# Moving the output projection, the second norm, the query products and the key scores between the two phases of units 1, 6, 7 and 8 in a gather-heavy transformer step

## The reference, cut to what matters

```
mod  = silu(cond) @ w_ada + b_ada                    # shift, scale, gate, twice
h    = rmsnorm(x) * (1 + scale1) + shift1
proj = h @ w_in                                      # recurrence inputs, query/key/value latents
hg   = gated linear recurrence, forward and backward, normed and gated
attn = 8 heads of attention over 128 cached + L own keys
x    = x + gate1 * (concat(hg, attn) @ w_out)        # "output projection"
h2   = rmsnorm(x) * (1 + scale2) + shift2            # "second norm"
q    = h2 @ peer_wq                                  # 8 heads x 2 halves x 128
s1, s2 = q_half1 . keys1, q_half2 . keys2            # "scores"
top 16 of each, top 16 of their 256 sums             # "choice": 128 experts per token
act  = gelu(h2 . u[idx])                             # 128 gathered rows of 1024 per token
x    = x + gate2 * sum_k(softmax_k * act_k * v[idx_k])
```

## Time and profile before

| | |
|---|---|
| median of 3 runs | 4956.92 us (4955.65 to 4961.89) |
| profiled execution | 4966.51 us |
| its span in the trace | 4963.9 us |
| TensorE busy | 3113.2 us, 63% |
| VectorE busy | 2887.5 us, 58% |
| GpSimd busy (issuing gathers) | 2860.5 us, 58% |
| moved by DMA | 1611.54 MB, mean 325 GB/s |
| mean granted TensorE clock | 0.792 |

### The profile page before, as it was taken

How to read it: one execution, slowest core, us unless ns; L and a number is a source line. 1 busy time by engine, 2 the same in 40 slices (tenths; PEclk the granted TensorE clock), 3 DMA queues, 4 the chain that set the end, 5 groups by cost and what they waited for, 6 DMA issues and landing times. The chain is left out here.

```text
span 4963.9 us, 51332 instructions
## 1 busy us (share of the span) xinstructions
PE 3113.2 (63%) x18926; PEld 1926.2 (39%) x18926; DVE 2887.5 (58%) x7102; ACT 596.3 (12%) x1287; POOL 2860.5 (58%) x2565
## 2 busy tenths in 40 slices
PE   6759587721777768457686853781178657657036
PEld 5555544520544554254264352350153531441001
DVE  1339773269346663776777469207825874784760
ACT  2211021200101111110011110310010100100000
POOL 0017573057555545764687756546656767767776
PEclk9679798665796689778998975895579689689569
DMA  6469795278899889998999987797789899999999
GB/s 217 145 197 332 255 347 195 67 249 275 293 419 367 332 306 383 361 419 341 380 385 389 394 340 266 274 361 258 271 309 409 317 406 417 340 419 419 345 414 372
DMA packets 447640, 1611.54 MB, mean 325 GB/s; under 512 B 55329, under 2 KB 57761, under 8 KB 445601
## 3 DMA queue, kind: packets, MB, share of 16 engines
q0 software_dynamic: 368640, 1342.34, 71.3%
q1 hardware_dynamic: 78752, 265.93, 14.5%
HBM read 1604.63 MB, written 3.44 MB: 324 GB/s over the span
## 5 line engine op out<-in xcount | busy, mean ns | idle before, releaser
L627 POOL DMA_INDIRECT ring<-in_peer_u,eidx x1280 | 1607.1, 1256 | 1289.1 <-DVE eidx L1457 593.4
L627 POOL DMA_INDIRECT ring<-in_peer_v,eidxT x1280 | 1253.1, 979 | 791.6 <-PE acc L914 454.1
L1481 DVE CUSTOM_DVE_ANT_0 ring<-ring,h 128x1024 f32<-128x1024 f32 x1280 | 1521.8, 1225 | 240.5 <-DMA ring<-in_peer_u,eidx 229.8
L914 PE MATMUL acc<-ring,wz 128*32 128x512 f32 x5120 | 1125.5, 624 | 238.0 <-DMA ring<-in_peer_v,eidxT 227.4
L914 PEld LDWEIGHTS acc<-ring,wz 128*32 128x32 f32 x5120 | 263.2, 112 | 925.8 <-issue 867.9
L867 PE MATMUL pp<-hT,wring 128*128 128x128 f32 x2560 | 342.6, 295 | 82.9 <-DMA wring<-in_w_q 82.6
L669 PE MATMUL tb<-ident,lat 128*128 128x128 f32 (+1 forms) x412 | 101.1, 394 | 435.6 <-DVE lat L1463 424.0
L867 PEld LDWEIGHTS pp<-hT,wring 128*128 128x128 f32 x2560 | 322.6, 207 | 125.4 <-DMA wring<-in_w_q 95.3
L711 PE MATMUL pp<-wring,hT 128*128 128x128 f32 (+1 forms) x2240 | 277.6, 287 | 34.9 <-DMA wring<-in_w_in 18.0
L711 PEld LDWEIGHTS pp<-wring,hT 128*128 128x128 f32 x2240 | 271.0, 203 | 51.7 <-DMA wring<-in_w_in 21.6
L839 PE MATMUL tb<-U,lat 128*128 128x64 f32 x672 | 150.1, 399 | 182.3 <-ACT lat L954 182.3
(11 more groups left out here) (196 smaller groups left out, 3315.3 us busy)
## 6 DMA issues: line engine op xcount, KB each, us to landing
wring<-in_w_q SPq DMA_DIRECT2D x160, 512.0 KB
wring<-in_w_in SPq DMA_DIRECT2D x125, 512.0 KB
wring<-in_w_ada SPq DMA_DIRECT2D x96, 512.0 KB
wring<-in_w_out SPq DMA_DIRECT2D x80, 512.0 KB
ring<-in_peer_u,eidx POOLq DMA_INDIRECT x1280, 6.4
ring<-in_peer_v,eidxT POOLq DMA_INDIRECT x1280, 7.0
wkvb<-in_keys SPq DMA_DIRECT2D x5, 1024.0 KB, 6.5
wqb<-in_wqb SPq DMA_DIRECT2D x4, 1152.0 KB, 11.4
```

Of the source, the lines that this page charges most:

```text
L627: pool.indirect_dma_start(ring[:, n % GR, :], None, A[table], bass.IndirectOffsetOnAxis(ap=rows, axis=0),).then_inc(s_g[n % GR], 16)
L914: ins = nc.tensor.matmul(acc[32 * q:32 * q + 32, half * 512:(half + 1) * 512], wz[:, at:at + 32], row[:, half * 512:(half + 1) * 512], sta ...
L1481: v.tensor_tensor_reduce(rows, rows, h2[:, u % 2, :], 1.0, 0.0, ALU.mult, ALU.add, dot[:, n:n + 1])\
```

## The change

Two functions cut the list `queries(p, t)` in two: `joined` is its first five steps (four `outp` and the `norm`), `searched` the rest (eight `wq` and the `score`). In units 1 and 6, `joined` leaves the v phase for the u phase. In units 7 and 8, `searched` leaves the u phase for the v phase. Units 0, 2, 3, 4, 5 and 9 stay as they are. No instruction is added or removed, and the order of the gathers and the order of the weight tiles stay the same; only their places against each other differ.

```diff
+def joined(p, t):
+
+    return queries(p, t)[:N_OUT // WCH + 1]
+
+
+def searched(p, t):
+
+    return queries(p, t)[N_OUT // WCH + 1:]
+
...
-    beside_u = {0: projections(1, 0, 20), 1: attention(1, 1),
+    beside_u = {0: projections(1, 0, 20), 1: attention(1, 1) + joined(1, 1),
...
-                6: attention(3, 1), 7: attention(3, 2) + queries(3, 2), 8: attention(3, 3) + queries(3, 3)}
+                6: attention(3, 1) + joined(3, 1), 7: attention(3, 2) + joined(3, 2), 8: attention(3, 3) + joined(3, 3)}
     beside_v = {0: scans(1, 0, 4),
-                1: queries(1, 1) + spread_pairs(choice(1, 1), modulations(1, 0, N_ADA // 2)),
+                1: searched(1, 1) + spread_pairs(choice(1, 1), modulations(1, 0, N_ADA // 2)),
...
-                6: queries(3, 1) + choice(3, 1), 7: choice(3, 2), 8: choice(3, 3),
+                6: searched(3, 1) + choice(3, 1), 7: searched(3, 2) + choice(3, 2), 8: searched(3, 3) + choice(3, 3),
```

## The result

The changed kernel takes 5021.34 us (median of 4 runs, 5004.39 to 5043.23), the kernel before 4956.28 us in the same comparison: ratio 1.014, 95% interval 1.0101 to 1.0178. It is slower by 65 us; 57 were forecast. The profiled execution is the fastest of the four, 5004.39 us with a span of 5001.9 us, 38 over that of before.

The account below looks back on a forecast made before the run. V phases were taken as bound by bytes, u phases by gather issue, the ends of units 1 and 6's u phases by the engine chain; 71 - 33 - 32 + 51 = +57 us on 4956.9 gave 5014, range 4968 to 5058.

Parts of the forecast that it names:

- Part A: Output projection and norm at the end of units 1 and 6's u phases: +35 us each, +71 together.
- The projection: Units 1 and 6, u phase's end: 64 products take 16.4 us, first three weight tiles loaded, DMA engines lightly loaded.
- an upper end: Units 1 and 6: +50 us each if the projection waits for weights as in unit 7, 25.0 us, or runs at half clock.
- The rival of the half clock: Units 1 and 6: projection at half clock or waiting for weights, 15 us more in each, 5044 us; chance 0.15.
- Part B: V phases of units 1 and 6 without output projection and norm: -17 us in unit 1, -16 in unit 6.
- Part C: U phases of units 7 and 8 without query products and scores: -18 us in unit 7, -14 in unit 8.
- attention stretch: Unit 7's u phase: 30 added gathers at unit 9's pace, 1.405 us each, +42 on 89.5, giving 131.7 us.
- the rest: Unit 7's u phase after attention: 25.7 MB, 62 us at 415 GB/s, issue 63 us; taken as 64.
- The rival that cancels: Units 7 and 8's u phases fall to 180 us, other parts at good ends: -5 us, 4952; chance 0.12.
- Part D: V phases of units 7 and 8 with query products and scores, 16 tiles: 189 us, +25.5 each, +51 together.
- The choice: V phases of units 7 and 8: begins at 43%, needs VectorE 73.69 us of some 107 left, so hidden.

Follow-up runs that it names:

- joined_1_6: The changed kernel with units 7 and 8 put back, so only units 1 and 6 differ from the kernel before; 4995.93 us against 4963.34, ratio 1.0086.
- searched_7_8: The changed kernel with units 1 and 6 put back, so only units 7 and 8 differ from the kernel before; 4994.87 us, ratio 1.0064.
- outp_only_1_6: As joined_1_6, but in units 1 and 6 the norm stays beside the v phase; 4974.02 us, ratio 1.0037.
- half_products: The kernel before with VectorE's products over 512 of the 1024 columns in units 7, 8 and 9; 4887.56 us, a single run.
- half_products_b: The same kernel as half_products, run again at the lower DMA rate; 5273.43 us, a single run.

## Why the prediction was right

**Part A, +35 in each.** Measured +33 and +38; the chain without cover is shown by joined_1_6, and by cover taking 34 us off it. Step by step in unit 6: gate row and transposes 5.7 for 5.9; from VectorE's first addition to the gelu product 3684.5 - 3668.6 = 15.9 for 16.2 (5.3 + 2.5 + 6.7 + 1.7). The projection was mis-sized: 24.1 for 16.4, near the 25.0 that I had named as an upper end; 6.2 us of it are waits for weight tiles. The reason given for the lower figure, lightly loaded DMA engines, was wrong: six gathers for the v phase are issued as the last products free the ring, and the weight tiles share the engines with them, which moved 414 GB/s while the fifth to seventh tile were used:

```profile
3655.40:3665.80 10.40, 7.41 (x48) 6.93 (x48) 0.00 (x0) 0.00 (x0) 1.17 (x2) 0.84 1.02 414
```

Most of that was made up by the heads: the last one's products began 3636.6 - 3373.2 = 263.4 us into the phase instead of 3640.1 - 3371.9 = 268.2, with fewer products between heads, 5 us that I had left out of the sum. The rival of the half clock didn't come: the first 48 products took 5.62 us, as in the earlier trace rows; the granted clock fell only to 0.84 over the row above, where 48 products took 7.44.

**Part B, -17 and -16.** Measured -14 and -24, -38 for -33. Right in sum, with one term missing: while VectorE waits, gathers for the v phase land that before landed in that phase itself. Unit 6's u phase moves 5.4 MB more than before (246 x 311.3 against 260 x 273.7) and its v phase 7.7 MB less (395 x 184.9 against 387 x 208.6), of which the eight tiles are 4.2.

**Part C, -18 and -14.** Measured -16 and -8 in the changed kernel, but -6 and 0 in searched_7_8. The same code gives phases of 207 to 217 us with the queries (before, joined_1_6, outp_only_1_6; mean of six 210.9) and of 200 to 210 without (changed kernel, searched_7_8; mean of four 205.2): the mean is 6 us each, not 16. Unit 7's 216.5 us, from which I subtracted, was the longest of the six. The windows of the changed kernel show unit 7's attention stretch and the rest, and GpSimd's group in the first:

```profile
3872.20:4000.10 127.90, 54.09 (x186) 39.99 (x185) 113.56 (x215) 15.83 (x38) 102.30 (x80) 0.53 0.93 327
4000.10:4069.80 69.70, 23.18 (x144) 21.52 (x144) 55.82 (x94) 8.00 (x15) 52.71 (x44) 0.63 0.98 384
```

```profile
L637 POOL DMA_INDIRECT ring<-in_peer_u,eidx x80 | 102.7, 1284 | 26.6 <-issue 24.1 <-DVE dot L1491 2.5
```

The stretch is right here: 127.9 for 131.7, at an issue of 1.28 us; in searched_7_8 it takes 136.7, at 1.41. The step that failed is "the rest": 45 x 1.405 = 63 us by the issue and 62 by the bytes. Without the query tiles it takes 69.7 us at 384 GB/s, not 415, with GpSimd at 1.20 us a gather and 0.3 between two, not 1.405 in all. Of the 69.7 us GpSimd waits for a buffer only 5.1, where it waited 23.3 of the 124.2 before. Once the bytes are out, the issue binds there too, and takes longer than in unit 9. For the attention stretch and unit 9 half_products shows the same limit; for the rest it is read from these waits alone.

The rival that cancels had as a reason that VectorE's work per gather falls by a third in attention. That is so only for attention's own instructions; all of VectorE's busy time falls from 79.80/53 = 1.51 to 113.56/80 = 1.42 us a gather, by 6%.

**Part D, +25.5 in each.** Measured +22 and +23: 16 tiles at 419 GB/s are 20. The whole phase ran at 417 and 409 GB/s; I had taken 398 for its first part from a piece of unit 6 that begins 54 us into that phase; why that piece was slower no run shows. Here the first part runs at 418, unlike unit 6's, where the DMAs start from a standstill (the third row, 368 over the first 85 us):

```profile
4074.80:4157.00 82.20, 70.56 (x484) 43.44 (x484) 0.00 (x0) 3.58 (x6) 48.46 (x52) 0.99 1.02 418
4157.00:4255.50 98.50, 76.31 (x332) 20.12 (x329) 73.38 (x302) 4.27 (x9) 73.29 (x77) 1.00 1.03 419
3684.50:3770.00 85.50, 74.09 (x478) 43.34 (x479) 0.29 (x1) 3.46 (x8) 46.49 (x50) 0.94 0.92 368
```

The choice was covered, as forecast.

So the mechanism was right in A, B and D, and the nearness of the sum is in part luck: errors of opposite sign stood in B and D (to the change's favour) and C (against it), and inside A between the projection and the heads. The two shares, 33 to 43 us for units 1 and 6 and some 31 for 7 and 8, stand against forecasts of 38 and 19.

**A version below the kernel before** is joined_1_6 with five chunks a head: 0.7% below in both measurements, and its traces agree: the u and v phases of units 1 and 6 (unit 1 counted from the end of unit 0) take 1193 and 1187 us in sum, against 1227 in half_products_b, where these units are those of the kernel before. The changed kernel with five chunks a head was 0.2 and 1.1% below, the first not clear of no change. Each was measured only where the kernel before took over 5200 us; where it takes 4960 nothing was measured.

## What to carry to other kernels

A step is cheap beside a phase only if that phase's limit isn't the step's own resource and if other work stands beside the step's whole chain: the chain behind the last head lengthened its phase by 38 us with nearly nothing beside it, and by 17 with more products beside it. Taking bytes out of a phase that is bound by the issue of its transfers gives back little, while the phase that takes them pays in full if it runs at the DMA engines' rate. Before weighing such a trade, find each phase's limit with a window, and check it at the DMA rate at which the kernel will run.

## What the runs showed of the hardware that was not expected

GpSimd's mean issue of a gather takes 0.94 us with half-width VectorE products and 1.03 to 1.13 with full ones in the same unit 9. The mean is made of issues of 0.94 us and single ones of up to 1.99. Unit 9's u phase, untouched and with nothing beside it, took 168, 173, 176, 180 and 181 us in five executions, the longer ones with the longer mean issue: what makes them differ from one execution to the next no run shows. And the v phase of unit 9 ran at 169 us in one set of runs and at 183 to 188 in others, where v phases without weights no longer fill the DMA engines in all cases (share 0.93 to 0.98 in units 7 and 8) and phases with them nearly do (0.98 to 1.00).
